# Prompt attention of a decoder step: the probabilities are transposed on VectorE, and the value products run as 32-row tiles in two parts per head

## The reference

```python
def block(args):                       # one block of 128 queries
    qn_b, qr_b, i = args
    sc = (jnp.einsum('bqhd,bkhd->bhqk', qn_b, k_nope)
          + jnp.einsum('bqhd,bkd->bhqk', qr_b, k_r)).astype(jnp.float32) * ATTN_SCALE
    q_pos = i * Q_BLOCK + jnp.arange(Q_BLOCK)
    sc = jnp.where(k_pos[None, :] <= q_pos[:, None], sc, -jnp.inf)
    p = jax.nn.softmax(sc, axis=-1).astype(v.dtype)
    return jnp.einsum('bhqk,bkhd->bqhd', p, v)
```

## Time and profile before

| | us |
|---|---|
| median of 3 runs | 1533.46 (1530.68 to 1536.91) |
| the profiled execution | 1532.18 |
| its span in the trace | 1530.5 |
| PE busy | 1505.8 (98%) |
| DVE busy | 934.7 (61%) |
| ACT busy | 551.6 (36%) |
| POOL busy | 243.8 (16%) |
| mean granted TensorE clock | 0.999 of full speed |

### The profile page before, as it was taken

The page is one execution under the profiler, slowest core; times in us unless marked ns, Lnnn a source line. Parts: engine busy times, 40 slices in busy tenths (PEclk is TensorE's granted clock), DMA queues, the critical chain, the costliest instruction groups (busy, mean ns, idle before and its releaser), DMA issues.

```text
span 1530.5 us, 32080 instructions
## 1 busy us (share of the span) xinstructions
PE 1505.8 (98%) x11757; PEld 1372.2 (90%) x11757; DVE 934.7 (61%) x1722; ACT 551.6 (36%) x1187; POOL 243.8 (16%) x431
## 2 busy tenths in 40 slices
PE   8999999999999999999999999999999999999998
PEld 7988888888887677778899999999999999999996
DVE  5675667666667788367664645554544545554557
ACT  5465665556664223232331312212131312112146
POOL 2010011101115541000030211212020311112000
PEclk9999999999999999999999999999999999999999
DMA  7112121111133998351220202022020202021003
GB/s 231 51 40 56 38 41 30 39 38 37 23 105 93 301 309 274 112 169 42 81 86 28 69 14 69 15 67 68 20 62 27 69 14 69 14 69 55 1 28 125
DMA packets 158655, 117.73 MB, mean 77 GB/s; under 512 B 55263, under 2 KB 145821, under 8 KB 158416
## 3 DMA queue, kind: packets, MB, share of 16 engines
q1 hardware_dynamic: 143280, 94.40, 20.9%
q10 hardware_dynamic: 11664, 11.44, 2.3%
q0 software_dynamic: 3600, 10.43, 2.1%
HBM read 106.08 MB, written 14.34 MB: 79 GB/s over the span
## 4 chain that ended last, share of the span: by engine, by line
PE 49%; DVE 1%; issue 0%; ACT 0%; DVEq 0%
PE banks L2120 16%; PE banks L2121 16%; PE banks L2122 16%; PE banks L2203 0%; PE banks L2205 0%; PE banks L2204 0%; PE banks L2190 0%; DVEq L1939 0%; DVE weight_stage L2523 0%; DVE down_stage L2523 0%; DVE weight_stage L2536 0%; DVE down_stage L2536 0%; DVE f_stats L2495 0%; ACT up_hi L2345 0%; ACT up_hi L2341 0%
## 5 line engine op out<-in xcount | busy, mean ns | idle before, releaser
L2120 PE MATMUL banks<-act_hi,up_hi 128*128 128x352 f32 (+2 forms) x1040 | 335.5, 323 | 0.8 <-PEq L1691 0.8
L2122 PE MATMUL banks<-act_hi,up_lo 128*128 128x352 f32 (+2 forms) x1040 | 335.4, 323 | 0.0
L2121 PE MATMUL banks<-act_lo,up_hi 128*128 128x352 f32 (+2 forms) x1040 | 335.1, 322 | 0.0
L2120 PEld LDWEIGHTS banks<-act_hi,up_hi 128*128 128x128 f32 x1040 | 195.3, 188 | 1.0 <-issue 1.0
L2121 PEld LDWEIGHTS banks<-act_lo,up_hi 128*128 128x128 f32 x1040 | 195.5, 188 | 0.0
L2122 PEld LDWEIGHTS banks<-act_hi,up_lo 128*128 128x128 f32 x1040 | 195.4, 188 | 0.0
L2423 DVE TENSOR_TENSOR o_t<-o_t,banks 128x352 f32<-128x352 f32 x240 | 121.0, 520 | 95.1 <-PE banks L2122 94.9
L2402 DVE SCALAR_TENSOR_TENSOR conv_out<-conv_in,conv_now,conv_out 128x1072 f32<-128x1072 f32 x42 | 64.7, 1540 | 185.2 <-ACT conv_out L2276 185.2
L1118 DVE TENSOR_REDUCE neg_max<-banks 128x1 f32<-128x896 f32 (+7 forms) x128 | 96.6, 755 | 105.5 <-PE banks L880 104.6
L2267 ACT ACTIVATE conv_in<-banks 128x352 f32<-128x352 f32 x84 | 36.4, 459 | 336.4 <-PE banks L2122 336.4
L2120 PE MATMUL banks<-gated_hi,down_hi 128*128 128x352 f32 x480 | 155.9, 325 | 0.0
(11 more groups left out here) (342 smaller groups left out, 3066.7 us busy)
## 6 DMA issues: line engine op xcount, KB each, us to landing
weight_stage<-in_w_f_up SPq DMA_DIRECT2D x44, 512.0 KB, 4.6
page_slot<-in_cache_kv_latent SPq DMA_DIRECT2D x100, 128.0 KB, 3.7
down_stage<-in_w_f_down SPq DMA_DIRECT2D x22, 512.0 KB, 4.3
page_slot<-in_cache_kv_latent ACTq DMA_DIRECT2D x51, 128.0 KB, 3.8
rope_rows<-in_cache_k_rope SPq DMA_DIRECT2D x256, 16.0 KB, 2.0
rope_slot<-rope_rows SPq DMA_DIRECT2D x16, 256.0 KB, 4.1
z<-in_x_prompt SPq DMA_DIRECT2D x8, 512.0 KB, 3.4
o_blocks<-o_t POOLq DMA_DIRECT2D x30, 128.0 KB, 2.2
```

The lines of the kernel that those rows point to most:

```text
L2120: nc.tensor.matmul(o, ws[0], xs[0], start=first, stop=False)
L2121: nc.tensor.matmul(o, ws[0], xs[1], start=False, stop=False)
L2122: return nc.tensor.matmul(o, ws[1], xs[0], start=False, stop=last)
```

## The change

The changed kernel does the following in `attend`.

- The units of a pair go head by head, and in a head through the query blocks 7, 0, 6, 1, 5, 2, 4, 3 (`UNITS`).
- DVE transposes the probabilities in blocks of 32 by 32 from SBUF to SBUF (`probs_t`). A block then has 32 keys on the partitions, and the quarter of the 128 partitions says which 32 queries of a query block it holds. The PE transposes and the copies after them are gone.
- The value products contract over 32 keys: 4 row tiles (the quarters) and 2 column tiles (even and odd blocks of keys), 128 products per head, with 32 to 256 columns (32 for each query block that sees the keys). They run in two parts per head (`values`, `VALUES_AT`), for head 0 at n = 10 and 11, for head 1 at n = 2 and 3 of the next pair. ACT copies the odd sum out (`o_odd`), DVE adds the even one (`o_sum`), POOL multiplies by the reciprocals (`o_done`).
- The values lie in SBUF once per quarter. They are transposed by DVE in blocks of 32 (`v_t`), stored to DRAM by SP, and loaded four times per head; `t0` and `t1` are gone.
- The reciprocals are taken for 8 query blocks at once, and PE transposes them spread over 64 columns, 8 per head.
- POOL takes the low halves of the queries (`q_low`) and of the weights; SP stores the results. The 256 gathers go in groups of four, with one read of the page table for four.
- The keys' halves are made head by head (`k_low(p, name, hh)`), so that head 1's are overwritten later.

```diff
-UNITS = [(g, hh, r) for g in (3, 2, 1, 0) for hh in range(2) for r in range(2)]
+UNITS = [(hh, t) for hh in range(2) for t in (7, 0, 6, 1, 5, 2, 4, 3)]
-OWN_AT = {0: "t0", 2: "t1", 3: "ql"}
-NEXT_AT = {4: "wt", 5: "v0", 6: "v1", 8: "k1", 9: "q02", 10: "q12", 11: "q01", 12: "q11", 14: "k0", 15: "q00", 16: "q10"}
-VALUES_AT = {5: (3, 0, 2), 7: (3, 2, 4), 9: (2, 0, 2), 11: (2, 2, 4), 14: (1, 0, 4)}
+OWN_AT = {0: ["q12", "q11"], 4: ["ql"], 5: ["q10"]}
+NEXT_AT = {6: ["wt", "q02"], 7: ["q01"], 8: ["q00"], 12: ["v0"], 13: ["k1", "k0"], 14: ["v1"]}
+INV_AT = {1: (1, 0), 3: (1, 1), 9: (0, 0), 11: (0, 1)}
+VALUES_AT = {2: (1, 0), 3: (1, 1), 10: (0, 0), 11: (0, 1)}
+OUT_AT = {4: 1, 12: 0}
+KEY_ORDER = [(0, 7, 1, 6), (2, 5, 3, 4)]
...
+            def values(p, hh, part):          # TensorE
+                if part == 0:
+                    pe.wait_ge(xt_ok, p * NU + 8 * hh + 8)
+                    pe.wait_ge(v_in[hh], (WD_IN if hh == 0 else 0) + 64 * (p + 1))
+                    if hh == 0 and p + 1 < PAIRS:
+                        taken(p + 1, "q00")
+                        taken(p + 1, "wt")
...
+                    elif p + 1 < PAIRS:
+                        taken(p + 1, "q11")
+                        taken(p + 1, "k0")
...
+                for jt in KEY_ORDER[part]:
+                    a, b = places_at(hh, jt)
+                    for half in range(2):
+                        for c in range(2):
...
+                            for i in range(4):
+                                r = slice(32 * i, 32 * i + 32)
+                                last = nc.tensor.matmul(ps[64 * c:64 * c + 64, 4 + i, 32 * a:32 * b], v[r, j, :], x[r, blocks, :],
+                                                        start=jt == 0 and half == 0, stop=part == 1 and jt == KEY_ORDER[1][-1] and half == 1)
...
+                elif name == "ql":            # bank_free: the wait ahead of a projection
+                    pe.wait_ge(iv_ok, 2 * head(p - 1, 1))
+                elif name == "v0":
+                    pe.wait_ge(iv_ok, 2 * head(p - 1, 0))
...
+                if n % 8 == 0:                # scores
+                    pe.wait_ge(kl_ok, k_count(p, "k0" if p else "k1", hh if p else 1))
...
+                elif n % 8 == 0:
+                    pe.wait_ge(ql_ok, q_count(p, "q10" if hh else "q00"))
...
+                for n in range(NU):           # ScalarE
+                    exp(p, n)
+                    if n in OUT_AT and (p or n > 4):
+                        o_odd(p - OUT_AT[n], OUT_AT[n])
...
+                    if n - 1 in INV_AT and (p or n > 4):
+                        inv_copy(p - INV_AT[n - 1][0], *INV_AT[n - 1])
+                    for q, name in units(p, n - 1):
+                        if name in BY_ACT:
+                            take(q, name)
+                        elif name[0] == "k":
+                            k_hi(q, name, 0)
+                        elif name[0] == "q":
+                            q_high(q, name)
...
                 for n in range(NU + 1):       # VectorE
+                    if n in (8, NU):
+                        inverse(p, n // 8 - 1)
+                    if n:
+                        probs_t(p, n - 1)
+                    if n in OUT_AT and (p or n > 4):
+                        o_sum(p - OUT_AT[n], OUT_AT[n])
                     if n + 1 < NU:
                         row_max(p, n + 1)
...
+                    for q, name in units(p, n - 1):
+                        if name[0] == "v":
+                            v_t(q, name)
+                        elif name[0] == "q" and name != "ql":
+                            q_scale(q, name)
+                    for q, name in units(p, n - 2):
+                        if name[0] == "k":
+                            k_low(q, name, 0)
...
-FIRST_KEYS_AT = {3 + i: (i // 5, KEY_PARTS[i % 5]) for i in range(10)}
+FIRST_KEYS_AT = {5 + i: (i // 5, KEY_PARTS[i % 5]) for i in range(10)}
```

More of the change, by code:

```diff
@@ L698, in proj_bank, with head, units, v_blocks @@
         def proj_bank(p, name):
[L699 to L703 removed]
+            return FIRST_BANK[name] if p == 0 and name in FIRST_BANK else BANK[name]
+        def head(p, hh):
+            return 2 * p + hh + 1
+        def units(p, n):
+            own = [(p, u) for u in OWN_AT.get(n, []) if p or u == "ql"]
+            return own + [(p + 1, u) for u in NEXT_AT.get(n, []) if p + 1 < PAIRS]
+        def v_blocks(p, hh):
+            return (vr if p + 1 < PAIRS else vr_last)[hh]
         def stage_free(eng):
[L706 to L707 removed]
+            eng.wait_ge(w.lo_ok, w.lo_count(PAIRS - 1, "q1"))
             eng.wait_ge(pj, pj_count(PAIRS - 1, "wt"))
+        def v_stored(eng, p):
+            eng.wait_ge(v_out, WD_IN + 64 * (p + 1))
         def scaled(eng):
@@ new lines, in gather @@
+            def gather(first, end):
+                for at in range(4 * first, min(4 * end, DEC_BATCH * N_PAGES), 4):
+                    f, b = at // 8, at % 8 // 4
+                    pages = nc.values_load_multi_w_load_instructions(m.pages[0:1, at:at + 4], [sp.engine])[1]
+                    for j, page in enumerate(pages):
+                        sp.dma_start(m.rope_rows[f // 2, :, f % 2, b, j, :],
+                                     io["cache_k_rope"][bass.ds(page, 1)].rearrange("o p c -> (o p) c")).then_inc(gathered, 16)
@@ new lines, in inverse_rows @@
+            def inverse_rows(p, hh, half):
+                bank = INV_BANK
+                pe.wait_ge(rv_ok, head(p, hh))
+                if hh and p + 1 == PAIRS:
+                    bank = 4 + half
+                    pe.wait_ge(sum_ok, head(p, 0))
+                elif half:
+                    pe.wait_ge(iv_ok, 2 * head(p, hh) - 1)
+                elif hh:
+                    taken(p + 1, "v0")
+                else:
+                    taken(p, "ql")
+                for i in range(4):
+                    at = 4 * half + i
+                    last = nc.tensor.transpose(ps[0:V_HEAD, bank, i * P:(i + 1) * P], rinv[:, hh, at:at + 1].to_broadcast([P, V_HEAD]), m.ident[:, :])
@@ new lines, in probs_t, with inverse, o_sum @@
+                a, wd = block_of(t, hh, 0), (t + 1) * P
+                out = x[:, a:a + wd // 32, :].rearrange("p j c -> p (j c)")
+                nc.vector.transpose(out, prob[n % 2][:, 0:wd]).then_inc(xt_ok, 1)
+            def inverse(p, hh):
+                dve.wait_ge(pr, p * NU + 8 * hh + 8)
+                if p:
+                    dve.wait_ge(fin, 2 * head(p - 1, hh))
+                nc.vector.reciprocal(rinv[:, hh, :], sums[:, hh, :]).then_inc(rv_ok, 1)
+            def o_sum(p, hh):
+                for half in range(2):
+                    dve.wait_ge(odd_ok, WD_IN + 2 * (head(p, hh) - 1) + half + 1)
+                    o = by_quarter(half)
+                    last = nc.vector.tensor_tensor(o, o, ps_half(0, half), ALU.add)
+                last.then_inc(sum_ok, 1)
@@ L1163, in _ @@
             q_scale(0, "q12")
-            q_low(0, "q02")
-            q_low(0, "q12")
+            q_low("q02")
+            q_low("q12")
+            v_t(0, "v1")
             q_scale(0, "q00")
@@ L1168, in _ @@
             row_max(0, 0)
+            q_low("q00")
+            q_low("q10")
             for p in range(PAIRS):
@@ L1201, in _ @@
                         keys_t(nc, dve, m, *FIRST_KEYS_AT[n])
-                if more:
-                    row_max(p + 1, 0)
             cached_max(nc, m, dve, 0)
-            o_done(PAIRS - 1, 0)
+            o_sum(PAIRS - 1, 1)
+            dve.wait_ge(sum_ok, 2 * PAIRS)
+            dve.wait_ge(iv_ok, 4 * PAIRS)
+            for half in range(2):
+                o = staged_o[:, half * 4 * P:(half + 1) * 4 * P]
+                last = nc.vector.tensor_tensor(o, o, iv[half], ALU.mult)
+            last.then_inc(of_ok, 1)
 NG = N_PAGES // 4
```

639 lines of the change are left out of this document (307 added, 332 removed).

## The result

The changed kernel took 1594.52 us in the median of four runs (1587.50 to 1604.52) against 1532.13 for the kernel before: a ratio of 1.0406, 95% interval 1.0342 to 1.0470. The forecast was 1546.0 with a range up to 1570. The sign was right, the size was not: +62 us where +12.5 had been forecast. The profiled execution is the fastest of the four, 1587.5 us with a span of 1585.8, so the traces differ by 55.3 us.

What follows compares the result with a forecast made beforehand. Attention was taken as bound by TensorE's slots, afterwards by hand-off waits: pair 0 41.3, six pairs 299.4, (a) 2.1, last pair 61.1, sum 403.9 against 391.4, +12.5, giving 1546.0 us; range 1508 to 1570, forecast's own 1536 to 1560.

Steps and rivals of the forecast that it cites:

- The seven waits: Middle pair, from one `v1` to the next: PE waits 16.8 us for other engines' results, 8.6 of them idle.
- (a): Ahead of a pair's first scores: PE waits 2.12 us for the next keys' low half, behind `v_t` of `v1`.
- PE's work falls from 49.1 to about 41.3: Middle pair: PE's work in us after removing transposes and old value products and adding inverse transposes and tiled products.
- eight tiles side by side: Value products: eight tiles work at the same time, so a part takes 2.4 or 2.2 us, 9.2 a pair.
- The rival with a floor between starts: Value products: eight can't start in under 0.20 us when widths change, +4.6 us a pair, 1583 in all; chance 0.06.
- what PE gains: Step pricing PE's removed and added work per pair, with the tiled value products at 9.2 us (bounds 8.9 to 10.1).
- idle time of PE was priced once: Middle pairs: 8.6 us of PE idle in a period of 49.9 us.
- and 1.5 of waits: Last pair: VectorE bounds it from the fifth unit, 27.6 us of work plus 1.5 of waits; the pair takes 61.1.
- the later stages' code stays: Stages after the attention: code unchanged, so the output projection was forecast to change by 0 us.
- Pair 0: First pair, without earlier values or own queries: 41.3 us from the first scores to the end of `v1`.
- SyncE's queue: Slower rival: 40 gathers at 0.98 us make the queue 57 us a pair, values' loads late, 1590; chance 0.06.
- break-even: Faster rival: the waits per middle pair, 14.9 us, at which the change gains nothing, last pair's price kept.

Runs made afterwards that it cites:

- the half products: Value products of odd key blocks left out of the changed kernel, 64 of 128 per part remaining: 1569.0 us in one profiled execution.
- the run with the three edits: Changed kernel with head 0's values loaded behind head 1's products, scaling ahead of row maximum, reciprocals' copy ahead of odd sum's, keys' low half first: 1544.3 us.

## Why the prediction was wrong

- **Right: the waits and what they are.** The seven waits of the path through a middle pair came at the forecast places, 8.1 us idle for 8.6; the period without disturbance was 51.3 for 49.9, inside the bounds of 49.1 to 52.7. Moving what I had named removed all of them but (a), of which 0.57 us stayed. The 1.4 us that are missing are PE's work: 43.1 us a pair where "PE's work falls from 49.1 to about 41.3", less half a microsecond of idle time.
- **Right: eight tiles side by side.** A part took 2.56 and 2.28 us from its first start to the next line's, for 2.4 and 2.2, 0.5 us a pair more than forecast; where the other 1.3 of PE's 1.8 us went wasn't followed. The rival with a floor between starts is refuted by the half products. The runs therefore side with the earlier trace rows, against the 60 cycles of the Trainium skill ("TensorEngine Tiling (Array Packing)", Instruction Overhead) as a floor per product here: 128 in 2.56 us are 20 ns each.
- **Wrong: "what PE gains" counted columns and not instructions.** The step priced 512 narrow products a pair at their time in the array. Their supply was left out: the profile of before shows a queue named instruction with 67 packets, and I never asked what twice the products of a pair do to it. The missed 13.0 us in six middle pairs (320.7 measured, 6 x 51.3 = 307.7 without disturbance) are four stalls with 6.2 us, and about 6.8 for 13.7 us at the lower clock, behind two of them and behind one wait (a). The cached scores, from which I took the price, have 144 such products in a row too, once in some 5 us, and showed one such stall themselves.
- **Wrong: idle time of PE was priced once.** The forecast gave PE 8.6 idle us a pair, and took the clock of the kernel before, which was hardly ever idle. Here the lower clock followed, 1.5 us for one gap of 2.02 in the half kernel, and 17 us at half speed in the last pair.
- **Wrong: "and 1.5 of waits" in the last pair.** It took 73.7 us for 61.1. VectorE's work was sized nearly right, about 30 us for 27.6 from 17.3 us in to its last transpose of probabilities, and the key transposes cost what they were priced. But that stretch took 40.5 us for 29.1, since VectorE stood idle in it for 10.8, waiting for PE's scores and ScalarE's copies: it wasn't the bound. PE stood still for two more instruction stalls (1.6 and 1.8), for 2.9 us ahead of scores(8), where the scaling stands behind key transposes, and for other hand-offs of 1.5 to 1.9, and ran at half speed from 511.2 to 528.3, which costs at most half of its 14.3 busy us. How these share the 12.6 us wasn't tested; the half kernel, without the stalls, took 68.2.
- **Wrong: "the later stages' code stays".** It did not: the result's rows are loaded as two halves of 64 partitions because head 1 lies in another order, part of the same diff. PE waited 4.5 us behind these loads, and the granted clock was at the lower level for 6.8 us from 722.9 on: 5.6 us in all.
- **Pair 0** took 45.6 us for 43.4 with wait (a). PE stood 3.8 us for the low half of the first queries, and the granted clock was at the lower level from 108.5 to 115.3, which is worth up to 3.4 us; no run tested it.
- **SyncE's queue** was a rival with a gather at 0.98 us; a gather took 0.72 to 0.80 us here, and up to 0.90 in the run with the three edits. It was no bound of the changed kernel, where it had some 3 us a pair to spare, and became the bound at 48 us a pair once the waits were mended. The rival named the right queue at a price that wasn't met.
- **A slip in the rivals:** break-even is at 16.8 less 12.5 / 6, so at 14.7 us of waits and not 14.9. Nothing rests on it.

Of the 55.3 us between the traces about 12.5 had been forecast. The rest is some 8.3 of undisturbed periods 1.4 longer, 13.0 of stalls and clock in middle pairs, 12.6 in the last pair, 5.6 in the output projection, 2.2 in pair 0, and 2 in decoding, whose first microseconds still run at the lower clock, less 0.6 at the start. The terms are read from one execution; in the slower runs of the four, which have no trace, how stalls and clock share the added 4 to 17 us stays open. Why a packet of instructions comes in time for one part of values and late for the next was not settled either: with less traffic there were two in the middle pairs for four, in one execution each, and half the instructions removed them.

## What to carry to other kernels

When a change trades few wide products for many narrow ones, count PE's instructions per microsecond beside its columns, and look among the DMA queues of the profile at what brings them. Price PE's idle time twice, once as a gap and once as the clock that it may cost behind it, and read a diff to its end: a new layout is paid for by every later stage that loads it. What an engine waits for in a hand-off is often only the order of two instructions on the other engine; here such edits, with one load moved, took the profiled time from 1587.5 to 1544.3 us.

## What the runs showed of the hardware

- 128 products on 32 by 64 tiles, of 256 to 32 columns, in groups of eight took 2.63 us, and 64 of them in groups of four 2.31: eight tiles cost hardly more than four.
- PE stood still for 0.3 to 3.4 us within a sequence of independent products, in every run that has all 128 of them, and went on 1.2 to 1.7 us after a 16 KB packet of instructions had ended; in the changed kernel these places lie whole multiples of 250 to 254 instructions apart.
- Eight products that nothing reads, put into a gap of 2.02 us, took 1.5 us off every second pair.
- With eight loads of 256 KB into 64 partitions the queues moved some 200 GB/s, and PE waited 4.5 us for what was queued behind them; with the same bytes as four loads of 512 KB into 128 partitions they moved some 300 GB/s, and PE waited 0.6 to 1.8 us.
